# Splitting the first weight chunks of a projection and of a merge on ACT and VectorE instead of GpSimd

## The reference, cut to what matters

```python
p = _split_in(x @ w_in[l])                 # first projection
ya, yb, yc, yd = ...                       # four mixers, 256 wide each
gates = sigmoid(p["gate"])                 # 4 x 1024, from x @ w_in as well
merged = sum over n of gates[n] * (y[n] @ w_branch[n])
x = layer_norm(ALPHA * x + merged @ w_out)
```

## Time and profile before

| | us |
|---|---|
| median of 3 runs | 3333.2 |
| lowest and highest | 3329.95, 3335.09 |
| the profiled execution, its time | 3336.09 |
| its span, first to last instruction | 3334.2 |
| PE busy | 2951.0 (89%) |
| DVE busy | 1739.5 (52%) |
| POOL busy | 1363.0 (41%) |
| ACT busy | 693.2 (21%) |

### The profile page before, as it was taken

One profiled execution on the slowest core, in us unless ns is written; L12 is line 12 of the kernel. 1 busy time (PEld: TensorE's weight loads), 2 busy tenths in 40 slices (PEclk: granted clock), 3 DMA queues, 4 the chain that ended last, 5 costly groups with the idle time before them and its releaser, 6 DMA issues. The chain is left out here.

```text
span 3334.2 us, 32888 instructions
## 1 busy us (share of the span) xinstructions
PE 2951.0 (89%) x12638; PEld 2187.2 (66%) x12638; DVE 1739.5 (52%) x2041; ACT 693.2 (21%) x1049; POOL 1363.0 (41%) x388
## 2 busy tenths in 40 slices
PE   6988776869769999669899998999898999989998
PEld 5843435747556666447468877887665578778877
DVE  3165454529356666456354546881353634468831
ACT  0022220011135555352240011000222410010000
POOL 5700000027301111213117776777432077667776
PEclk9978887969969999879899999999999899999999
DMA  3322110014238888512202222222232022222223
GB/s 137 127 92 74 44 41 35 1 66 143 82 122 327 319 333 314 227 63 95 62 14 101 89 89 88 89 101 89 103 106 75 1 85 92 88 85 92 101 89 114
DMA packets 85185, 366.43 MB, mean 110 GB/s; under 512 B 32174, under 2 KB 32558, under 8 KB 46744
## 3 DMA queue, kind: packets, MB, share of 16 engines
q1 hardware_dynamic: 66088, 338.55, 27.7%
q10 hardware_dynamic: 7696, 17.21, 1.5%
q0 software_dynamic: 11232, 8.43, 0.8%
HBM read 364.75 MB, written 36.08 MB: 120 GB/s over the span
## 5 line engine op out<-in xcount | busy, mean ns | idle before, releaser
L133 POOL TENSOR_TENSOR w_hi<-w_raw,w_zero 128x2048 fp32r<-128x2048 f32 x142 | 512.1, 3606 | 1261.8 <-DVE yl L639 820.6
L176 PE MATMUL bank<-xh,w_hi 128*128 128x512 f32 x1704 | 678.8, 398 | 96.9 <-POOL w_lo L136 34.3
L136 POOL TENSOR_TENSOR w_lo<-w_raw,w_hi 128x2048 fp32r<-128x2048 f32 x142 | 666.9, 4697 | 11.1
L177 PE MATMUL bank<-xl,w_hi 128*128 128x512 f32 x1704 | 670.4, 393 | 0.0
L178 PE MATMUL bank<-xh,w_lo 128*128 128x512 f32 x1704 | 670.1, 393 | 0.0
L176 PEld LDWEIGHTS bank<-xh,w_hi 128*128 128x128 f32 x1704 | 324.1, 190 | 193.7 <-issue 51.2
L178 PEld LDWEIGHTS bank<-xh,w_lo 128*128 128x128 f32 x1704 | 324.3, 190 | 69.0
L177 PEld LDWEIGHTS bank<-xl,w_hi 128*128 128x128 f32 x1704 | 325.0, 191 | 66.4 <-issue 1.5
L152 POOL TENSOR_TENSOR w_lo<-w_raw,w_hi 128x2048 fp32r<-128x2048 f32 x22 | 102.9, 4679 | 260.6 <-ACT w_hi L146 260.6
L2574 DVE TENSOR_TENSOR fl<-work,fh 128x512 fp32r<-128x512 f32 x44 | 202.2, 4595 | 1.5
L711 DVE SCALAR_TENSOR_TENSOR res<-res,bank 128x512 f32<-128x512 f32 x40 | 27.5, 688 | 315.6 <-PE bank L178 315.6
(11 more groups left out here) (538 smaller groups left out, 5049.3 us busy)
## 6 DMA issues: line engine op xcount, KB each, us to landing
w_raw<-weights SPq DMA_DIRECT2D x216, 1024.0 KB, 4.8
raw<-weights SPq DMA_DIRECT2D x51, 1024.0 KB, 8.7
res<-weights SPq DMA_DIRECT2D x26, 1024.0 KB, 6.2
early_gates<-gate_rows SPq DMA_DIRECT2D x20, 256.0 KB, 2.1
ahead<-early_gates ACTq DMA_DIRECT2D x20, 256.0 KB, 3.1
distance_bias<-distance_bias_once ACTq DMA_DIRECT2D x8, 512.0 KB
na_bias<-grid_bias SPq DMA_DIRECT2D x16, 240.0 KB, 4.6
strips<-distance_bias SPq DMA_DIRECT2D x8, 448.0 KB, 3.2
```

What stands on the lines that cost most here:

```text
L133: pool.tensor_tensor(self.hi[:, s, :], self.raw[:, s, :], self.zero[:, 0:1].to_broadcast([128, CHUNK]), ALU.add).then_inc(self.rounded, 1)
L136: pool.tensor_tensor(self.lo[:, s, :], self.raw[:, s, :], self.hi[:, s, :].bitcast(F32), ALU.subtract).then_inc(self.split, 1)
L176: self.released(pe.matmul(out, hi, moving[0], start=start, stop=False))
L177: pe.matmul(out, hi, moving[1], start=False, stop=False)
```

## The change

At the start of the kernel ACT issues x as one DMA, rounds the first chunk, waits for x, rounds its eight tiles, and then issues the three DMAs for constants and parameters and rounds the second chunk. VectorE subtracts the first chunk, then the tiles of x. GpSimd waits until VectorE has split all of x, subtracts the second chunk, and divides from the third on. In the first merge (the one with early gates) ACT rounds two chunks ahead of the mixers' outputs, VectorE subtracts the first ahead of its other work, and GpSimd subtracts the second once the mixers' outputs are split. `subtract` takes any engine and an end. The blocks for GpSimd are written behind those for VectorE, as both count `n_split` on while the program is made.

```diff
--- before.py
+++ after.py
@@ -145,13 +145,14 @@
             act.wait_ge(self.used, self.turn + (c - SLOTS + 1))
         act.activation(self.hi[:, s, :], self.raw[:, s, :], ACT.Copy).then_inc(self.rounded, 1)
 
-    def subtract(self, pool):
-        for c in range(self.n_split, self.to_split):
+    def subtract(self, engine, upto=None):
+        upto = self.to_split if upto is None else upto
+        for c in range(self.n_split, upto):
             s = c % SLOTS
-            pool.wait_ge(self.rounded, self.turn + (c + 1))
-            pool.tensor_tensor(self.lo[:, s, :], self.raw[:, s, :], self.hi[:, s, :].bitcast(F32),
-                               ALU.subtract).then_inc(self.split, 1)
-        self.n_split = self.to_split
+            engine.wait_ge(self.rounded, self.turn + (c + 1))
+            engine.tensor_tensor(self.lo[:, s, :], self.raw[:, s, :], self.hi[:, s, :].bitcast(F32),
+                                 ALU.subtract).then_inc(self.split, 1)
+        self.n_split = upto
 
     def take(self, pe, n=1):
 
@@ -300,15 +301,21 @@
     names = ("zeroed", "consts_in", "x_in", "rounded_x", "split_x")
 
     def scalar(act, zeroed, consts_in, x_in, rounded_x, split_x):
+        act.dma_start(k.res[:, :, :], k.dram["xT"]).then_inc(x_in, 16)
+        k.ws.round(act, 0)
+        act.wait_ge(x_in, 16)
         for t in range(KT):
-            act.dma_start(k.res[:, t, :], k.dram["xT"][:, t, :]).then_inc(x_in, 16)
+            act.activation(k.xh[:, t, :], k.res[:, t, :], ACT.Copy).then_inc(rounded_x, 1)
         act.dma_start(k.consts[:, :], k.dram["consts"]).then_inc(consts_in, 16)
         act.dma_start(k.par1[:, :], k.dram["params1"]).then_inc(consts_in, 16)
         act.dma_start(k.mats1[:, :], k.dram["mats1"]).then_inc(consts_in, 16)
+        k.ws.round(act, 1)
         act.wait_ge(consts_in, 48)
 
-    def gpsimd(pool, zeroed, *_):
+    def gpsimd(pool, zeroed, consts_in, x_in, rounded_x, split_x):
         pool.wait_ge(zeroed, 1)
+        pool.wait_ge(split_x, KT)
+        k.ws.subtract(pool, 2)
 
     def tensor(pe, t, zeroed, consts_in, x_in, rounded_x, split_x):
         pe.wait_ge(split_x, t + 1)
@@ -320,10 +327,8 @@
         dve.memset(k.eps[:, 2:3], 64e-5).then_inc(zeroed, 1)
         dve.memset(k.eps[:, 3:4], 1.0).then_inc(zeroed, 1)
         dve.memset(k.eps[:, 4:5], 1e-5 / ALPHA ** 2).then_inc(zeroed, 1)
+        k.ws.subtract(dve, 1)
         for t in range(KT):
-            if t == 0:
-                dve.wait_ge(x_in, 16 * KT)
-            dve.tensor_copy(k.xh[:, t, :], k.res[:, t, :]).then_inc(rounded_x, 1)
             dve.wait_ge(rounded_x, t + 1)
             dve.tensor_tensor(k.xl[:, t, :], k.res[:, t, :], k.xh[:, t, :].bitcast(F32), ALU.subtract).then_inc(
                 split_x, 1)
@@ -362,12 +367,6 @@
                 first_run["scalar"](act, *first_sems)
             if "scalar" in aside_run:
                 aside_run["scalar"](act, *aside_sems)
-
-        @block.gpsimd
-        def _(pool):
-            if "gpsimd" in first_run:
-                first_run["gpsimd"](pool, *first_sems)
-            ws.divide(pool)
 
         @block.tensor
         def _(pe):
@@ -408,6 +407,12 @@
                 for q in range(nt):
                     last = dve.tensor_copy(rows[:, q, :], k.bank[4 + q][:, 0:width])
                 last.then_inc(rows_copied, 1)
+
+        @block.gpsimd
+        def _(pool):
+            if "gpsimd" in first_run:
+                first_run["gpsimd"](pool, *first_sems)
+            ws.divide(pool)
 
 
 @contextmanager
@@ -568,6 +573,7 @@
     with memory(k, yh=("r", KT, SEQ), yl=("r", KT, SEQ), mh=("r", KT, SEQ), ml=("r", KT, SEQ), sig=(2, SEQ),
                 part=(2, SEQ), ahead=(4 if early else 1, SEQ)) as (yh, yl, mh, ml, sig, part, ahead):
         ws.plan(KT * len(late) + 8 * KT)
+        first = ws.n_split
         with stage(k, "gate_ready", "sigmoid_ready", "branch_ready", "banks_free", "branch_rounded", "merge_order",
                    "branch_split", "x_in", "ahead_in0", "ahead_in1", "ahead_in2", "ahead_in3") as (
                 block, gate_ready, sigmoid_ready, branch_ready, banks_free, rounded, order, branch_split, x_in,
@@ -579,11 +585,6 @@
                 ws.load(sp)
                 if x_dram is not None:
                     sp.wait_ge(x_in, 16)
-
-            @block.gpsimd
-            def _(pool):
-                pool.wait_ge(branch_split, KT)
-                ws.divide(pool)
 
             @block.tensor
             def _(pe):
@@ -614,6 +615,9 @@
 
                 for e in range(min(4, len(early))):
                     ahead_load(e)
+                if early:
+                    ws.round(act, first)
+                    ws.round(act, first + 1)
                 for t in range(KT):
                     act.activation(yh[:, t, :], k.yb[:, t, :], ACT.Copy).then_inc(rounded, 1)
                 for u in range(4 * KT):
@@ -634,6 +638,8 @@
             @block.vector
             def _(dve):
                 step = Order(dve, order)
+                if early:
+                    ws.subtract(dve, first + 1)
                 for t in range(KT):
                     dve.wait_ge(rounded, t + 1)
                     dve.tensor_tensor(yl[:, t, :], k.yb[:, t, :], yh[:, t, :].bitcast(F32), ALU.subtract).then_inc(
@@ -652,6 +658,13 @@
                         if n:
                             step(dve.tensor_tensor(part[:, 0, :], part[:, 0, :], part[:, 1, :], ALU.add))
                     step(dve.tensor_tensor(ml[:, dt, :], part[:, 0, :], mh[:, dt, :].bitcast(F32), ALU.subtract))
+
+            @block.gpsimd
+            def _(pool):
+                pool.wait_ge(branch_split, KT)
+                if early:
+                    ws.subtract(pool, first + 2)
+                ws.divide(pool)
         add_product(k, KT, mh, ml, scale_residual, eps, part)
```

## The result

The changed kernel took 3309.83 us in the median of four runs (3308.71 to 3313.28) against 3334.14 for the kernel before (3329.95 to 3337.53): a ratio of 0.9929, 95% interval 0.9912 to 0.9947, so 24 us or 0.7% faster. The forecast was 3309.2. Measured again beside other kernels it took 3313.23 against 3336.37, 0.9928 (0.9914 to 0.9942). Its first profiled execution took 3313.28 with a span of 3311.4, 22.8 under the span of before.

The account below looks back on a forecast made before the run. GpSimd's chunk splitting was taken to bound stage starts, TensorE or VectorE later stretches. Gains of 13.1 (start), 9.6 (merge) and 1.3 (table load) sum to 24.0 us, giving a 3309.2 us median, range 3303 to 3314, chance 0.77.

Parts of the forecast that it names:

- both places: Kernel start and first merge: nothing is split yet, so GpSimd's rounding and splitting, some 8.3 us a chunk, is not hidden.
- The start: Kernel start: first matmul at 16.5 us, third chunk's rounding at 30.9 instead of 44.02, 13.1 us gained (11.1 to 14.6).
- a late x: Kernel start: x landing at 17.1 us as before would put the first matmul at 18.5, the range's late end.
- the gain at the start taken back: Rival at the start: chunk lands at 14.2, first matmul 19.2, gain 10.4, total 3312; chance 0.04, including the gain absorbed later.
- the step of 14.4 us: Kernel start: the third chunk's rounding begins 14.4 us after the first matmul, with TensorE running from a cold clock.
- asked for near 20 us: Kernel start: constants requested near 20 us, used by nobody in this stage; their 1.8 MB take 4.5 us.
- Covers: Spare time before TensorE needs the second split chunk: 3.6 us at the start, 1.4 us in the merge.
- rival with a late second chunk: Start and merge: TensorE waits for the second chunk; 5 to 10 us lost, 3314 to 3319; chance 0.10.
- The table load: Between the stages, at the head norm: ACT's load moves to the start and is hidden, 1.3 us gained (0 to 1.3).
- The merge: First merge: TensorE starts at 717.0 instead of 726.59, 9.6 us gained (8.0 to 10.5).
- VectorE's lock: Middle of the merge: VectorE's operations held beside GpSimd keep their distances; VectorE was busy 78.42 of 80 us.
- rivals in which it fell otherwise: SBUF lock holds VectorE more: in this merge, up to 3327, chance 0.06; in all merges and layers' products, 3342 to 3349, 0.03.

Follow-up runs that it names:

- third version: Changed kernel with start loads ordered on one queue, ACT's merge roundings ahead of its four DMAs, second-chunk rounding ahead of constants' DMAs; 3304.06 us, 0.9896 of the kernel before.
- version with ordered loads: Changed kernel with first chunk, two halves of x, bias rows and second chunk loaded in that order on SyncE's queue; 3303.75 us against 3333.58 before, 0.9924.
- run with GpSimd first: Changed kernel with GpSimd instead of VectorE subtracting the first chunk at the start, and no hold there; 3319.69 us in one execution.

## Why the prediction was right

**What bounds the kernel:** both places stood as read. The start's gain and the merge's are independent and reach the end whole.

**The start:** the mechanism was right, one term of the sum mis-sized. I put the first matmul at 16.5 (ends 15.0 and 18.5); it came at 18.54, at the far end, and the gain at the third chunk was 11.3 instead of 13.1. The step that failed is the landing of the chunk, put at 9.4 to 12.4 us: it was 13.6. x, on the other hand, was there at 10.4 (0.75 + 9.6), where I had 14.2. So the far end of my range was met by the other chain than the one I had given for it, a late x. It is the rival of the gain at the start taken back, with its chunk at 14.2 and a gain of 10.4, that came near. The large pieces of x did take share, as the experiment with small ones confirmed, and the rule cited from the Trainium skill (DMA: Bandwidth & Descriptors, Queues, rings and completion order), read as an even share, put the chunk at 9.4 and the first matmul at 15.5: the trace disagrees by 4 us and 3 us. What I left out of the working are the bias rows, which I counted by their bytes alone. Of the chunk's sixteen increments fourteen came by 11.8 us and the last two at 13.5 and 13.6, as the second chunk's did behind the rows in the third version, and the DMA engines were not full meanwhile (same columns as the earlier trace rows):

```profile
12.00:14.00 2.00, 0.00 (x0) 0.00 (x0) 0.00 (x0) 0.36 (x1) 0.00 (x0) 1.00 0.62 258
```

With x in small pieces the fourteen were in by 9.6 and the last two at 12.1 and 12.4. So x's share would have cost the chunk some 2.2 us and put it at 11.8, and the first matmul, 4.9 behind it as measured, near 16.7, an estimate; the rest of the delay is the two late parts. No run moves the rows alone behind the first chunk, so that split is argued from these records; x, the rows and the second chunk all moved behind it bring it to 5.8. From the first matmul on, the step of 14.4 us to the third chunk's release was 14.2; it took 13.2 and 14.4 in other runs, by when TensorE's clock rose.

**Constants:** "asked for near 20 us" was wrong. They went out at 13.68, as ACT's queue issued them ahead of the activations written before them. And I priced their new place at nothing by itself: issued early they cost 4.6 us. Most of that fell on the two late parts of the first chunk, which came at 18.2 instead of 13.6; the other fourteen were in by 13.6 instead of 11.8. The sum didn't need that, since in it the landing had been taken without them.

**Covers:** the second chunk was ready at 27.43 (predicted 26.8), about 5 us ahead of need rather than 3.6, as TensorE itself was later. In the merge it was ready at 714.17 with 0.7 us of cover instead of 1.4. The rival with a late second chunk did not happen.

**The table load:** 1.28 us, as said, and shown alone. The Trainium skill (ScalarE activation tables: per-element evaluation and per-set limits, Table sets in the compiler and the runtime) speaks of loads placed per block; here neither the first square of the next stage nor the merge's copies had one. Of the further 1.3 us up to the indexer 0.9 are the clock's and 0.4 are open; the prediction had neither.

**The merge:** 9.6 predicted, 9.7 in the trace, 10 (5 to 16) alone. VectorE's lock kept its distances: 78.42 us in both windows. The rivals in which it fell otherwise, in one merge or in all, did not happen.

**The sum:** 24.0 predicted; by the marks 23.5, by medians 24.3 and 23.1. That 3309.2 was met within 1 us is luck, as a single execution spreads by more: the start gave 1.8 less than its term, an unforeseen 1.3 came in at the norm, and the same kernel's second measurement was 3.4 higher.

## What to carry to other kernels

At the start of a program, and of each stage that begins with nothing split, write down in which order the first engine needs its bytes, and put the loads on a queue in that order, with what nobody needs yet behind them; here that was worth another 8 us of a first matmul, 6 of them still there at the third chunk, after the split had been moved to the faster engines. A load of a few rows counts by more than its bytes: ahead of a chunk it cost 4 us here. Work handed to GpSimd beside VectorE's operations of two SBUF operands made whichever started second longer, 0.9 to 4.3 us at a time; that mattered only where TensorE waited for it. A DMA written behind activations on ACT's queue was not issued behind them: if it has to wait, make the queue wait for something.

## What the runs showed that I had not expected

- ACT's DMAs ran ahead of its activations: the constants were issued at 13.68 us, with 6 us of rounding that stands before them in the program still to come; at 10.99 in the version with ordered loads. Behind a wait they did stand back: at 17.26 behind the one for x in eight pieces, which landed then, and at 17.35 behind the one for the second chunk's landing.
- A load of 0.14 MB in 34 rows, in front of a chunk in the same queue, delayed it from 13.1 to 17.3 us. Between 12 and 14 us the DMA engines showed as busy in both, with 256 GB/s moved instead of 389. Fourteen of the chunk's sixteen parts were in by 14.3.
- Eight pieces of 256 KB for x landed at 17.2 us, one of 2 MB at 10.4, beside the same chunk loads.
- Without the hold, at the start, GpSimd's subtraction began at 21.93 among VectorE's of x: it took 5.49 us instead of 4.60, and VectorE's took no longer. In the merge it began at 705.80, ahead of VectorE's first at 706.21, and one of VectorE's took 4.76 us; in the run with GpSimd first one took 5.02. That agrees with what the Trainium skill (SBUF — State Buffer, SBUF: two separate sides) says of a lock taken by who starts first.
